# A mixture-of-experts layer on one core: weights split into two halves on chip, a ring of three split units, and the last two blocks combined by selection products

## What is computed

```python
logits = (h @ w_router) + b_router            # 8 experts
top_p, top_i = lax.top_k(softmax(logits), 2)  # the two best, renormalised
for e in range(8):
    out = out + gates[..., e:e + 1] * ((silu(h @ w1[e]) * (h @ w3[e])) @ w2[e])
x = x + out
```

## Time and profile before

| | us |
|---|---|
| median of 3 runs | 3526.97 |
| lowest and highest run | 3516.93, 3528.78 |
| the profiled execution | 3521.7 |
| its span, first to last instruction | 3519.8 |
| PE busy | 3026.6 |
| DVE busy | 1632.7 |
| ACT busy | 984.5 |

### The profile page before, as it was taken

How to read it: one execution, slowest core, us unless ns; L and a number is a source line. 1 busy time by engine, 2 the same in 40 slices (tenths; PEclk the granted TensorE clock), 3 DMA queues, 4 the chain that set the end, 5 groups by cost and what they waited for, 6 DMA issues and landing times.

```text
span 3519.8 us, 42047 instructions
## 1 busy us (share of the span) xinstructions
PE 3026.6 (86%) x17332; PEld 2515.0 (71%) x17332; DVE 1632.7 (46%) x3308; ACT 984.5 (28%) x1680; POOL 327.4 (9%) x459
## 2 busy tenths in 40 slices
PE   3998688888789999998989688888888699999996
PEld 2988577778788999998889577768888444444442
DVE  4767566665554433346675567665554100000001
ACT  1343244443333212122432344443333000000010
POOL 3000122220000000000000222220000100000001
PEclk9999788778789999998999778878889799999998
DMA  4212100002222222222222000002221689999995
GB/s 150 89 60 74 33 8 16 8 1 86 69 88 72 73 73 84 77 71 76 61 61 72 23 16 9 8 9 90 96 78 31 241 297 316 315 318 319 316 314 182
DMA packets 219182, 385.15 MB, mean 109 GB/s; under 512 B 34534, under 2 KB 156454, under 8 KB 218992
## 3 DMA queue, kind: packets, MB, share of 16 engines
q1 hardware_dynamic: 202640, 329.80, 28.6%
q0 software_dynamic: 16352, 52.67, 4.3%
HBM read 352.99 MB, written 29.44 MB: 109 GB/s over the span
## 4 chain that ended last, share of the span: by engine, by line
PE 69%; DVE 17%; ACT 7%; issue 4%; POOL 2%; DMA 1%; POOLq 0%; DVEq 0%; ACTq 0%
PE ACC L353 15%; PE ACC L355 14%; PE ACC L354 14%; PE ACC L757 13%; PE TP L757 6%; DVE TR L1376 2%; PE TP L507 2%; DVE XC L1343 1%; DVE WL L1165 1%; PE TP L778 1%; DVE PTL L1193 1%; PE TP L353 1%; PE ACC L522 1%; PE TP L354 1%; PE TP L355 1%
## 5 line engine op out<-in xcount | busy, mean ns | idle before, releaser
L353 PE MATMUL ACC<-XH,WH 128*128 128x288 f32 x1984 | 596.2, 300 | 40.0 <-DVE XP L1244 36.7
L355 PE MATMUL ACC<-XH,WL 128*128 128x288 f32 x1984 | 596.7, 301 | 0.0
L354 PE MATMUL ACC<-XL,WH 128*128 128x288 f32 x1984 | 595.6, 300 | 0.0
L757 PE MATMUL ACC<-MW,XT 128*128 128x512 f32 x1024 | 445.7, 596 | 1.1 <-ACT XT L1121 1.1
L353 PEld LDWEIGHTS ACC<-XH,WH 128*128 128x128 f32 x1984 | 381.4, 192 | 43.5 <-DVE WL L1165 43.1
L813 ACT ACTIVATE WH<-RAW 128x2048 fp32r<-128x2048 f32 (+1 forms) x129 | 238.3, 1847 | 537.5 <-PE ACC L355 530.0
L354 PEld LDWEIGHTS ACC<-XL,WH 128*128 128x128 f32 x1984 | 381.3, 192 | 0.0
L355 PEld LDWEIGHTS ACC<-XH,WL 128*128 128x128 f32 x1984 | 379.5, 191 | 0.0
L757 PEld LDWEIGHTS ACC<-MW,XT 128*128 128x128 f32 x1024 | 194.5, 191 | 241.0 <-issue 239.5
L1165 DVE TENSOR_TENSOR WL<-RAW,WH 128x2048 fp32r<-128x2048 f32 (+1 forms) x129 | 284.2, 2203 | 108.5 <-ACT WH L813 108.3
L1784 DVE SCALAR_TENSOR_TENSOR HT<-HT,ACC 128x1024 f32<-128x1024 f32 x16 | 19.5, 1221 | 657.4 <-ACT HT L1127 657.4
(11 more groups left out here) (454 smaller groups left out, 5846.0 us busy)
## 6 DMA issues: line engine op xcount, KB each, us to landing
MW<-in_moe_w_dram SPq DMA_DIRECT2D x192, 1024.0 KB, 6.1
RAW<-in_w_in_dram SPq DMA_DIRECT2D x36, 1024.0 KB
RAW<-in_ffn_w_dram SPq DMA_DIRECT2D x30, 1024.0 KB
dispatched<-ZT POOLq DMA_DIRECT2D x4, 2048.0 KB, 17.6
RAW<-in_w_out_dram SPq DMA_DIRECT2D x8, 1024.0 KB
RAW<-in_w_mk_dram SPq DMA_DIRECT2D x8, 1024.0 KB
RAW<-in_w_mv_dram SPq DMA_DIRECT2D x8, 1024.0 KB
RAW<-in_w_mq_dram SPq DMA_DIRECT2D x8, 1024.0 KB
```

What stands on the lines that cost most here:

```text
L353: nc.tensor.matmul(out, a[0], b[0], start=first, stop=False)
L354: nc.tensor.matmul(out, a[0], b[1], start=False, stop=False)
L355: return nc.tensor.matmul(out, a[1], b[0], start=False, stop=last)
L757: mm = nc.tensor.matmul(out[:, h, :], lhs[:, 2 * pair + j, :], MW[n % RING][:, j, h * 512:(h + 1) * 512], start=(pair, j) == (0, 0), stop= ...
```

## The change

- Each of the 192 units is split on chip: ACT writes the high half and DVE the low half into one of three buffer pairs (WH and WL twice, and WH3/WL3), and PE makes three fp32r products for each product. The two operands XT and GT become pairs too (XTH/XTL, GTH/GTL), with the low parts made by DVE out of PSUM.
- The raw ring has six places instead of ten; a place is free when DVE has made the low half. The last six units use four of them, because two lie in XN, into which the gathers write. Units 0 to 3 may be loaded before the dispatch; unit 4 and all later ones wait for it.
- The order of the splits on ACT and DVE is written out by hand between the steps of a block.
- Blocks 0 to 7 belong to experts 0 to 7, so their expert number is a constant; the rows beyond 128 of an expert go to blocks 8 and on, with four more small steps on DVE (FAR). The numbers that were loaded as IOT come from a product of ones with the triangle.
- The router is made in two halves, the first ahead of the norm sums.
- Blocks 14 and 15 are not stored. Their results stay on chip as a pair, DVE builds a selection matrix of zeros and ones for each before the blocks start (ten small steps of 128 x 128, turned by PE, copied by ACT), and PE brings them back to token order with it (`back_to_tokens`); DVE adds them to TOK with gates that are zero elsewhere. Their rows in `returned` are zeroed at the start of the kernel.
- The gathers of the other blocks are issued before the end: the first choice of all five token tiles, then the second into the same buffer.

```diff
-RING = 10
+RING = 6
+SPLITS = 3
+LATE = BLOCKS - 2
...
+def raw_place(n):
+    return n % RING if n < len(UNITS) - RING else n % RING % 4
+def raw_before(n):
+    return max((k for k in range(n) if raw_place(k) == raw_place(n)), default=None)
...
+def following(b):
+    return ups(b + 1)[0:3] if b + 1 < BLOCKS else downs(b)
...
+        WH3, WL3 = put("WH3", [P, UNIT], F32R), put("WL3", [P, UNIT], F32R)
+        SELT = [put("SELT0", [P, T], F32R)]
...
+        FINAL = [(at("YH0", [P, D], F32R, XB_AT), at("YL0", [P, D], F32R, XB_AT + 4 * D)),
+                 (at("YH1", [P, D], F32R, XT_AT), at("YL1", [P, D], F32R, XT_AT + 4 * D))]
+        SPLIT = [(WH[:, 0], WL[:, 0]), (WH[:, 1], WL[:, 1]), (WH3[:], WL3[:])]
+        XL_AT = B0 - 2 * 4 * UNIT
+        RING_AT = [XL_AT, XL_AT + 4 * UNIT, RAW0, RAW0 + 4 * UNIT, XN_AT, XN_AT + 4 * UNIT]
         MW = [at("MW%d" % k, [P, 2, D], F32, offset) for k, offset in enumerate(RING_AT)]
-        YG = at("YG", [P, TT, D], F32, A0)
...
+                pe.sem_inc(s["x_low_free"], 1)
...
+                    def router(chunks):
+                        bank = open_tp()
+                        for tt in range(TT):
+                            for c in chunks:
+                                mm = nc.tensor.matmul(bank[0:rows(tt), tt * EXPERTS:(tt + 1) * EXPERTS], XG[:, c, tt * P:tt * P + rows(tt)],
+                                                      RW[:, c, :], start=c == chunks[0], stop=c == chunks[-1])
+                        mm.then_inc(s["tp_ready"], 1)
+                    pe.wait_ge(s["router_in"], 32)
+                    pe.wait_ge(s["x_hi"], 6 * C - 4)
+                    router((0, 1, 2, 3))
                     norm_sums()
-                    bank = open_tp()
-                    for tt in range(TT):
-                        for c in range(C):
-                            mm = nc.tensor.matmul(bank[0:rows(tt), tt * EXPERTS:(tt + 1) * EXPERTS], XG[:, c, tt * P:tt * P + rows(tt)],
-                                                  RW[:, c, :], start=c == 0, stop=c == C - 1)
-                    mm.then_inc(s["tp_ready"], 1)
+                    pe.wait_ge(s["x_hi"], 6 * C)
+                    router((4, 5, 6, 7))
...
+                    def halved_unit(key, out, lhs, last):
+                        n, pair = TURN[key], key[2]
+                        pe.wait_ge(s["m_lo"], n + 1)
+                        wh, wl = (w.rearrange("p (j h n) -> p j h n", j=2, h=2) for w in SPLIT[n % SPLITS])
                         for j in range(2):
                             for h in range(2):
-                                mm = nc.tensor.matmul(out[:, h, :], lhs[:, 2 * pair + j, :], MW[n % RING][:, j, h * 512:(h + 1) * 512],
-                                                      start=(pair, j) == (0, 0), stop=(pair, j) == (3, 1))
+                                c = 2 * pair + j
+                                mm = product(out[:, h, :], (lhs[0][:, c, :], lhs[1][:, c, :]), (wh[:, j, h, :], wl[:, j, h, :]),
+                                             c == 0, c == last)
                         mm.then_inc(s["m_used"], 1)
...
+                    def back_to_tokens(j):
+                        high, low = FINAL[j]
+                        for tt in range(TT):
+                            n = j * TT + tt
+                            if n >= 2:
+                                pe.wait_ge(s["c_free"], n - 1)
+                            for h in range(2):
+                                out, mine = ACC[0:rows(tt), n % 2, h, :], SELT[j][:, tt * P:tt * P + rows(tt)]
+                                nc.tensor.matmul(out, mine, high[:, h * 512:(h + 1) * 512], start=True, stop=False)
+                                mm = nc.tensor.matmul(out, mine, low[:, h * 512:(h + 1) * 512], start=False, stop=True)
+                            mm.then_inc(s["c_done"], 1)
...
-                    expert_down(BLOCKS - 1)
+                    pe.wait_ge(s["m_gt"], BLOCKS)
+                    pe.wait_ge(s["m_y"], BLOCKS - 1)
+                    down_piece(BLOCKS - 1, (0, 1))
+                    back_to_tokens(0)
+                    down_piece(BLOCKS - 1, (2, 3))
+                    pe.wait_ge(s["m_y"], BLOCKS)
+                    back_to_tokens(1)
...
+                    def halve(keys):
+                        for key in keys:
+                            n, k = PLACE[key], TURN[key]
+                            act.wait_ge(s["mw%d" % raw_place(n)], 16 * raw_turn(n))
+                            if k >= SPLITS:
+                                act.wait_ge(s["m_used"], k - SPLITS + 1)
+                            fn(SPLIT[k % SPLITS][0], MW[raw_place(n)][:].rearrange("p j n -> p (j n)"), ACT.Copy).then_inc(s["m_hi"], 1)
...
+                        if b >= LATE:
+                            fn(FINAL[b - LATE][0][:], pairs(TP[:, 2:4]), ACT.Copy).then_inc(s["m_yh"], 1)
...
+                    halve(ups(0)[0:3])
+                    t.skip("acc", 1 + TT)
+                    for j in range(2):
+                        m = t.next("acc")
+                        act.wait_ge(s["acc_ready"], m.n)
+                        fn(SELT[j][:], pairs(ACC[:, m.slot(2)])[:, 0:T], ACT.Copy).then_inc(s["acc_free"], 1)
+                        act.wait_ge(s["acc_free"], m.at(2))
...
+                        halve(ups(b)[3:8])
+                        halve(downs(b - 1)[0:2] if b else following(b)[0:2])
                         gate_tanh(b)
+                        halve(downs(b - 1)[2:4] if b else following(b)[2:3])
                         if b + 1 < BLOCKS:
                             input_turned(b + 1)
                         if b:
+                            halve(following(b)[0:3])
                             block_out(b - 1)
                         hidden_turned(b)
+                    halve(downs(BLOCKS - 1)[3:4])
...
+                    step(v.tensor_scalar(FAR[:], RANK[:, 0:TT, :], float(P), None, ALU.is_ge))
+                    step(v.tensor_tensor(FAR[:], FAR[:], e8(NB[:, 3, :], TT), ALU.mult))
+                    step(v.tensor_tensor(FAR[:], FAR[:], iota, ALU.add))
...
+                    for j in range(2):
+                        step(v.tensor_scalar(PSB[:, j], PS[:], -float((LATE + j) * P), None, ALU.add))
+                        if j:
+                            dve.wait_ge(s["acc_ready"], t.last("acc"))
+                        for tt in range(TT):
+                            ins_ = v.tensor_scalar(SEL[:, tt, :], IOT[:], PSB[:, j, 0, tt:tt + 1], None, ALU.is_equal)
+                        step(ins_)
+                        for tt in range(TT):
+                            ins_ = v.scalar_tensor_tensor(out=SEL[:, tt, :], in0=IOT[:], scalar=PSB[:, j, 1, tt:tt + 1], in1=SEL[:, tt, :],
+                                                          op0=ALU.is_equal, op1=ALU.add)
+                        ins_.then_inc(s["sel"], 1)
+                        t.skip("acc", 1)
...
+                    def halve_low(keys):
+                        for key in keys:
+                            k = TURN[key]
+                            dve.wait_ge(s["m_hi"], k + 1)
+                            high, low = SPLIT[k % SPLITS]
+                            v.tensor_tensor(low, MW[raw_place(PLACE[key])][:].rearrange("p j n -> p (j n)"), high.bitcast(F32), ALU.subtract)\
+                                .then_inc(s["m_lo"], 1)
...
+                    def out_low(j):
+                        high, low = FINAL[j]
+                        dve.wait_ge(s["m_yh"], j + 1)
+                        v.tensor_tensor(low[:], pairs(TP[:, 2:4]), high[:].bitcast(F32), ALU.subtract).then_inc(s["m_y"], 1)
+                    def add_late(j):
+                        for tt in range(TT):
+                            n, r = j * TT + tt, rows(tt)
+                            dve.wait_ge(s["c_done"], n + 1)
+                            v.scalar_tensor_tensor(out=TOK[0:r, tt, :], in0=pairs(ACC[:, n % 2])[0:r], scalar=GB[0:r, j, tt:tt + 1],
+                                                   in1=TOK[0:r, tt, :], op0=ALU.mult, op1=ALU.add).then_inc(s["c_free"], 1)
+                    halve_low(ups(0)[0:3])
+                    input_low(0)
+                    for b in range(BLOCKS):
+                        halve_low(ups(b)[3:8])
+                        halve_low(downs(b - 1)[0:2] if b else following(b)[0:2])
+                        gated(b)
+                        halve_low(downs(b - 1)[2:4] if b else following(b)[2:3])
+                        if b + 1 < BLOCKS:
+                            input_low(b + 1)
+                        if b:
+                            halve_low(following(b)[0:3])
+                            if b - 1 >= LATE:
+                                out_low(b - 1 - LATE)
+                        hidden_low(b)
+                    halve_low(downs(BLOCKS - 1)[3:4])
+                    add_late(0)
+                    dve.wait_ge(s["c_free"], TT)
+                    for k in range(TOP_K):
```

(80 more changed lines are left out.)

114 lines of the change are left out of this document (75 added, 39 removed).

## The result

The changed kernel takes 3399.59 us (median of 4 runs, 3397.94 to 3402.2), the kernel before in the same comparison 3526.38 (4 runs, 3516.93 to 3528.78). The ratio is 0.9646, with a 95% interval of 0.9627 to 0.9665: faster, 3.5%. The forecast was 3389, range 3362 to 3430. The span fell from 3519.8 to 3397.9 us, by 121.9.

A forecast was written before the change was run, and what follows sets the result against it. PE bounds the kernel. Start at 2779.3, blocks 0 and 1, then 14 blocks of 35.0 us reach 3323.8; a 58 us tail gives span 3381.8, profiled 3384, plus 5.3 for the median: 3389 us, range 3362 to 3430.

The forecast's parts named there:

- The bound and the product: Expert blocks: PE ends last at 0.231 us a product, 35.0 us a block, DVE and DMA 2 to 3 us behind.
- DMA at 367 GB/s: Rival for the blocks: DMA becomes the bound, 37.1 us a block, 3421 us in all; chance 0.13.
- The ring stalls PE: Rival for the blocks: longer handovers in the ring of three make PE wait, +2.1 us a block, 3421; chance 0.13.
- Products nearer 0.215: Rival for the blocks: faster products leave DVE the bound at 33.5 us a block, 3366 in all; chance 0.08.
- Two passes for a half: Rival for the blocks: each half costs two passes like a whole fp32 word, 61.8 us a block; chance 0.01.
- The clock: Rival for the blocks: PE falls to the low clock half of the time, 46.7 us a block, 3570; chance 0.04.
- The head: Before the blocks: earlier router half, faster dispatch landing and first input start up(0) at 2779.3, 15 us earlier (bounds 3 to 20).
- From up(0) to T: Blocks from up(0) at 2779.3 to the end of up(15) at 3323.8, including 14 blocks of 35.0 us.
- The tail: From the end of up(15) to the end of the kernel: 58 us instead of 60.8, bounds 50 and 66.
- the tail gets 1 us for it: Tail: down(15)'s third unit gets its slot at T+5.95, is needed at T+11.1, 1 us less than a landing.
- the clock behind the forecast's own hole: Tail: after a 6.8 us PE hole down(15) starts at T+18.8; only block 15's later products were put at the low clock.
- the second trip of the gathers: Tail: second-choice gathers, issued as XN rows come free, take 4.45 us each from issue to add, to T+45.

The follow-up runs named there:

- the single wait in the kernel before: Kernel before the change, with SP loading no expert unit until the dispatch has landed: 3505.06 us, ratio 0.996.
- gathers held back: Changed kernel, with POOL issuing the ten gathers only once down(15)'s third unit has landed: 3391.27 us in this single run.
- again: The changed kernel run again with no edit, 5 runs: 3400.53 us, ratio 0.9654.
- the adds in the hole: Changed kernel, with DVE's five first-choice adds moved ahead of the last low half and the gathers left early: 3386.02 us, ratio 0.9609.
- the ring of two: Changed kernel with two split buffers per ring instead of three, the order of the halvings moved accordingly: 3594.73 us, one run.
- two products: Changed kernel with two of each unit's three products, leaving out the one with the low half of the tokens' operand: 3355.99 us, one run.
- four raw slots: Changed kernel with four raw slots for all units instead of six: 3425.65 us, one run.
- half the low words: Changed kernel with two of three products, and DVE making only half of each low half, which PE uses twice: 3345.79 us, one run.

## Why the prediction was right, and which term was mis-sized

**The bound and the product.** Right. The forecast took 0.231 us from the earlier trace rows and 35.0 a block; it was 0.2326 and 35.23. The Trainium skill (TensorE: Matmul & The Clock Gate, "Back-to-back issue gap") gives about 216 ns for isolated products of 512 columns and 131 measured in a stream; these fp32r products are 8% above the first, and no stretch of them comes near the second. That DVE, ACT and DMA keep up was right too: DVE worked 271 and ACT 226 of 300 us, DMA moved 387 GB/s where 410 are to be had, and units landed in 7.6 us, under the 12 asked for.

**The rivals.** DMA at 367 GB/s: wrong, 387 is what PE asks for and 410 is to be had. The Trainium skill (DMA: Bandwidth & Descriptors, "Bandwidth") has about 358 GB/s a core as what binds transfers from HBM, and beside it 425 measured with the other core of the pair idle. This case's traces hold 387 and 410 over 300 us on one core, which disagrees with the 358 as a bound and is in line with the 425. The ring stalls PE: not with three slots, and by 12.4 us a block with two. Products nearer 0.215: no, 0.2326. Two passes for a half: no, by the same rows. The clock: 1.00 in the blocks.

**The head.** up(0) was forecast at 2779.3 and came at 2779.64, in part by errors that cancel, so the hit is partly luck. The dispatch had landed at 2767.6. The forecast says 2768.6, but its own terms (2765.81 less 3, plus 1 for the small steps and 4 for the landing) make 2767.8; in the trace the last issue ended 3.07 earlier and the landing took 4.88; the first input then took 7.23 (forecast 5), and with that its low half, not DVE's earlier steps, was the last to be ready. That the dispatch had landed so late because of the weight loads beside it is shown by the single wait in the kernel before: 17.88 to 4.88.

**From up(0) to T.** T was forecast at 3323.8, measured 3330.4. Three terms make the 6.6: up(0) ends 1.2 us late; block 0 to block 1, forecast 30.3, took 32.46, because the transposes behind PE's hole of 6.55 us took 1.94 in place of 0.87 and the first products behind them stood 0.43 apart, at a granted clock of 0.50, where the forecast had reckoned with the full clock; and 14 blocks by 0.23 are 3.2.

**The tail** is the step that failed: forecast 58 us with an upper bound of 66, measured 67.5. From T, in us, for the two traces of the changed kernel and the single run with the gathers held back:

| | forecast | measured | again | gathers held back |
|---|---|---|---|---|
| down(15) starts | 18.8 | 23.2 | 20.6 | 18.7 |
| last low half ends | 25.8 | 32.8 | 29.8 | 28.5 |
| add_late(0) done | 32.3 | 39.1 | 36.1 | 34.8 |
| first choice added | 38.7 | 45.2 | 42.2 | 40.9 |
| second choice added | 45 | 54.2 | 51.5 | 49.8 |
| last add | 54.5 | 64.1 | 62.1 | 60.0 |
| end | 58 | 67.5 | 65.5 | 63.4 |

Three terms were mis-sized. The first is "the tail gets 1 us for it": the late third unit was given the 6.1 us landing of the old blocks, where it took 10.55, with 2.4 MB of gathers beside it. That is 4.4 us, the whole delay of down(15) in this execution, but 1.8 in the other, and with the gathers held back down(15) starts as forecast. The tail is 5.4 us too long even then, so this term is not the main one.

The second is the clock behind the forecast's own hole. It put block 15's selection products at the low clock after idle PE, and gave down(15) the full clock behind a hole of 6.8 us, without a reason. In all three traces the first products of down(15) stand 0.43 us apart instead of 0.23, and the last halving has to wait for them: 9.5, 9.2 and 9.8 us from the start of down(15) to the last low half, where the forecast has 7.0. That is 2.2 to 2.8 us.

The third is the second trip of the gathers: 9.0, 9.3 and 8.8 us from the last first-choice add to the last second-choice one, in place of 6.3, so 2.5 to 3.0. It was priced by the 4.45 of the earlier trace rows for each tile, which is the first gather of ten. The trace of the kernel before had another price in the same place, in its chain of waits, for a later gather:

```profile
3504.46 9.33 DMA XN<-returned,PSI
```

In the changed kernel the gather that DVE waits for last needs 6.52.

For the profiled execution the three make 4.4 + 2.5 + 2.7 = 9.6 of the 9.5; what else differs cancels. What the prediction did see, that DVE's order and not the new products sets the tail, the adds in the hole confirm: they take 11 to 13 us out of it.

**What the time owes to luck.** The span was 16.1 us longer than the sum, 6.6 in the blocks and 9.5 in the tail; the median came only 10.6 above 3389. The difference is the 5.3 us that the forecast added because the profiled execution before was faster than the median of its kernel. The one after was not faster than its own (3399.62 and 3399.59), so that term was not needed and hides a third of the error.

## What to carry to other kernels

When work is added on several engines at once, list for one period what each must do (here PE 35.2, DMA 33.0, DVE 32.4, ACT 27.1) and then follow one slot of the ring that couples them: a ring is deep enough when its round, with handovers, fits into the other slots' work, and one slot too few can cost more than the whole change gains. Price a transfer by the traffic that will be beside it, not by its landing elsewhere. Behind every hole of several microseconds that a forecast itself puts into PE, look up at which clock the rows have the products that follow such a hole. Where an engine idles before a step that waits, look whether something further down its program is already ready: moving five adds there took 11 to 13 us out of the tail.

## What the runs showed of the hardware

A small hole before each unit did not cost the clock. In the ring of two PE was busy 246 of 300 us and the granted clock was 0.96, near its upper level of 2.4 GHz, with waits of some 0.7 us; in attention, at 42.85 of 50 us, it was 0.80. One long hole did: behind 5.78, 6.42, 6.55 and 10.36 us of idle PE the products of 512 columns stood 0.43 us apart at a granted clock of 0.50, the 1.2 GHz level; behind one of 3.03 us, in the kernel with the adds alone, 0.23 at 1.00.

DMA was not used up at a share of 1.00: 387 GB/s in the changed kernel, 410 at a share of 1.03 with two products, both over 300 us. What a 1 MB weight unit needs to land, median over the same 300 us, went with the rate: 5.0 us at 283 GB/s (ring of two), 7.2 at 373 (four raw slots), 8.0 at 387 (changed kernel), 11.1 and 13.5 at 410 (two products, without and with half the low words). The number of raw slots differs in one of these, four instead of six.

Executions whose programs are the same up to the tail differ by up to 11 us in where block 0 stands (first tanh at 2796.99 in one, 2808.22 in another) and by 0.2 us from there to the sixteenth: most of the scatter between these traces is made ahead of block 0. What makes it wasn't tried.
